# A hybrid attention step on one core: forgetting and differential score tasks mixed, gate products spread by VectorE's work, first attention pieces loaded early

## Chip, cores and metric

One NeuronCore of a Trainium2 chip runs the whole kernel. The metric is the device time of one execution in microseconds; lower is better. All operands are float32; matrix products are made of three products of halves (a high part, which the array takes without loss, and the low rest), so that one product of 128x128 by 128x512 appears as three matmuls.

## The reference

One decoder layer for a prompt of 2048 rows and for 8 sampled sequences of 4 rows. The prompt's part that matters here:

```python
q_a, k_a, v_a, gate_a, q_b, k_b, v_b, f_b, gate_b, m_a, m_b = split(h @ w_in)
# differential attention: 4 heads, two maps each, 64 wide, causal, linear position bias
s = einsum('bqmhd,bkmhd->bmhqk', q, k) * DH_A ** -0.5
p = softmax(where(dist >= 0, s - slopes * dist, NEG_INF))
p = p[:, 0] - lam * p[:, 1]
o_a = einsum('bhqk,bkhd->bqhd', p, v)
# forgetting attention: 8 heads, 64 wide, causal, bias from sums of log forget values
s = q @ k * DH_B ** -0.5 + F_q - F_k
o_b = softmax(where(causal, s, NEG_INF)) @ v
y = (sigmoid(m_a) * y_a + sigmoid(m_b) * y_b) @ w_o     # gates: columns of h @ w_in
```

## The kernel before, in words

The stages follow one another: `head` and `project` twice (one per half of the rows) make queries, keys, values and part of the gates. Then come `gates_and_maps`, `attention_a` (differential), `attention_b` (forgetting), `sample` and `merge`. The change lies in `gates_and_maps` and in the start of `attention_a`.

`gates_and_maps` (L1660) does three things at once. **Gate products:** six chunks of 512 columns by eight row tiles of 128, 24 matmuls each (L2115), 1152 in all; ScalarE copies a finished tile out of one of two PSUM banks `z` (L1922) and issues its store (L1930). Weights of a chunk come in two halves, `front` (two places) and `back` (one place). **Forgetting tasks,** 192 of them: a score tile of 128 rows by up to 1024 columns (L2068, one matmul per 512 columns) of which only the row maximum is kept, by VectorE: L1982 for whole tiles, L1979 with the causal mask for diagonal ones. **Differential tasks,** 192 of them, over 64 map rows (4 heads by 16 row tiles): for map m = 0 and 1 the score tile of each half kh of the keys (L2086 and L2087, two matmuls per 512 columns), its maximum (L1993, L1996), the exponentials on ScalarE (L1942), the row sums' factor (L2003 to L2007), and the difference p0 - factor x p1 (L2016), which SyncE stores to DRAM as the final map (L1834). A row tile of the first eight has one half, the others two.

Score tiles live in six PSUM banks; a tile of 1024 columns takes two. A bank of a forgetting tile comes free with its maximum, one of a differential tile with its exponential. TensorE works through the products in order, and each task has a written-out due product (`due`): the task's matmuls are issued before that product. Before the change all forgetting tasks come first, then all differential ones, and `due` comes from a small model of VectorE's pace (`dve_of`, `paced`). ScalarE follows the same due times, VectorE the order of tasks. The difference of map row g-1 stands behind the maximum of task (m = 1, kh = 0) of row g.

SyncE issues all loads and the maps' stores in one order, written per forgetting segment of eight tasks and per map row: weights that are due, keys and queries for later tasks (after a wait for the scores that used their places), then the stores of the previous row's map pieces (after the wait for its difference). Map pieces p0 have a ring of five, p1 of two.

`attention_a` (L2123) loads each map again in 40 blocks of 512x512 (L2166; a diagonal block in four copies, 640 KB; another 1 MB) into eight places, turns them on TensorE (L2263), splits them in high and low parts on ScalarE (L2225) and VectorE (L2247), and multiplies by the values (L2283, L2284, L2290). An output of four tiles is scaled (L2239) and stored. Its SyncE queue also loads values (`load_v`, 1 MB per part) and the first two units of `attention_b` (`load_b`, 3.1 MB each, behind blocks 8 and 14).

## Time and profile before

| | us |
|---|---|
| runs (median of 3) | 2637.28 (2634.48 to 2637.7) |
| profiled execution | 2636.46 |
| its span in the trace | 2634.8 |
| `gates_and_maps` (first product to last) | 943.6 to 1551.7 |
| `attention_a` up to the first score of `attention_b` | 1551.7 to 1762.3 |

The span is that of the engines' instructions; the profiled execution took 1.7 us more.
### The profile page before, as it was taken

What the parts mean: (1) busy time and instruction counts of PE and PEld (TensorE: products, weight loads), DVE (VectorE), ACT (ScalarE), POOL (GpSimd) and SP (SyncE); (2) the same over time, 40 slices, a digit from 0 to 9 for tenths busy, and PEclk for the clock granted to TensorE, in tenths of its full rate; (3) what the DMA queues carried; (4) which work ended last, traced back from release to release, by engine and by line L of the source; (5) the groups of instructions that cost most, each with busy time, mean ns of one, the idle gap of its engine ahead of it and who ended that gap; (6) DMA issues with size and microseconds to landing.
All of it is one profiled execution on the core that took longest, in us unless ns stands there. A gap on an engine that the chain in (4) does not pass through costs nothing. (4 is left out here: it accounts for less than half of the span.)

```text
span 2634.8 us, 34403 instructions
## 1 busy us (share of the span) xinstructions
PE 2447.5 (93%) x12466; PEld 1942.9 (74%) x12466; DVE 1549.1 (59%) x2701; ACT 837.6 (32%) x1445; POOL 185.4 (7%) x182
## 2 busy tenths in 40 slices
PE   6999999999999999999887677999999987999998
PEld 2788888887788877887665456887777754788886
DVE  3412246634666258887678744557787755655564
ACT  4211122234323210034444433444444433321221
POOL 1000122201222000000000011000000000000000
PEclk8999999999999999999995569999999999999999
DMA  8644645464454563456664569943546298554542
GB/s 315 232 162 173 213 124 170 153 216 157 142 157 125 202 200 129 142 185 211 208 205 138 165 194 287 322 137 77 123 97 138 88 339 293 173 143 152 154 126 65
DMA packets 323812, 463.19 MB, mean 176 GB/s; under 512 B 61929, under 2 KB 201073, under 8 KB 312574
## 3 DMA queue, kind: packets, MB, share of 16 engines
q1 hardware_dynamic: 309810, 419.79, 52.2%
q10 hardware_dynamic: 12800, 41.36, 4.1%
q8 instruction: 87, 1.43, 0.2%
q0 software_dynamic: 1056, 0.13, 0.1%
q14 instruction: 59, 0.48, 0.1%
HBM read 288.15 MB, written 173.04 MB: 175 GB/s over the span
## 5 line engine op out<-in xcount | busy, mean ns | idle before, releaser
L709 PE MATMUL proj_z<-first_km,h_hi 128*128 128x512 f32 x576 | 231.0, 401 | 3.2 <-DVE first_v L1274 3.2
L1942 ACT ACTIVATE max_p<-max_s_ps,max_neg_top 128x1024 f32<-128x1024 f32 (+4 forms) x192 | 164.7, 862 | 198.9 <-DVE max_neg_top L1993 149.6
L709 PE MATMUL proj_z<-first_km,h_lo 128*128 128x512 f32 x576 | 227.5, 395 | 0.0
L709 PE MATMUL proj_z<-first_v,h_hi 128*128 128x512 f32 x576 | 227.3, 395 | 0.0
L2086 PE MATMUL max_s_ps<-max_k,max_q 128*128 128x512 f32 (+3 forms) x320 | 148.3, 465 | 73.8 <-ACT max_p L1942 42.5
L709 PE MATMUL proj_z<-proj_w_hi,h_hi 128*128 128x512 f32 x512 | 203.2, 397 | 0.0
L709 PE MATMUL proj_z<-proj_w_hi,h_lo 128*128 128x512 f32 x512 | 199.9, 390 | 0.0
L709 PE MATMUL proj_z<-proj_w_lo,h_hi 128*128 128x512 f32 x512 | 199.3, 389 | 0.0
L2385 ACT ACTIVATE att_b_pf<-att_b_s_ps 128x1024 f32<-128x1024 f32 (+2 forms) x160 | 142.6, 898 | 101.1 <-PE att_b_s_ps L2428 77.6
L2402 DVE TENSOR_TENSOR att_b_p_lo<-att_b_pf,att_b_p_hi 128x1024 fp32r<-128x1024 f32 (+2 forms) x160 | 170.5, 1066 | 5.5
L2086 PEld LDWEIGHTS max_s_ps<-max_k,max_q 128*128 128x128 f32 x320 | 76.6, 240 | 111.6 <-ACT max_p L1942 59.4
L2087 PE MATMUL max_s_ps<-max_km,max_qm 70*128 70x512 f32 (+3 forms) x320 | 140.8, 450 | 0.0
L2397 DVE CAST att_b_p_hi<-att_b_pf 128x1024 fp32r<-128x1024 f32 (+2 forms) x160 | 98.0, 613 | 68.8 <-ACT att_b_pf L2385 66.3
L2247 DVE TENSOR_TENSOR att_a_p_lo<-att_a_turned,att_a_p_hi 128x512 fp32r<-128x512 f32 (+3 forms) x160 | 93.5, 607 | 74.5 <-ACT att_a_p_hi L2225 74.0
L1049 POOL TENSOR_TENSOR proj_rstd<-proj_rstd,keep_neg_half 128x8 f32<-128x8 f32 (+1 forms) x68 | 112.6, 1655 | 325.4 <-DVE proj_rstd L1372 325.4
L709 PEld LDWEIGHTS proj_z<-first_km,h_hi 128*128 128x128 f32 x576 | 108.4, 188 | 28.9 <-issue 5.0
L709 PEld LDWEIGHTS proj_z<-first_km,h_lo 128*128 128x128 f32 x576 | 108.3, 188 | 25.6
L709 PEld LDWEIGHTS proj_z<-first_v,h_hi 128*128 128x128 f32 x576 | 108.5, 188 | 23.9
L1240 ACT ACTIVATE proj_work<-proj_z 128x512 f32<-128x512 f32 x64 | 38.2, 597 | 272.8 <-PE proj_z L709 272.8
L1370 DVE TENSOR_REDUCE proj_ss<-proj_work 128x8 f32<-128x512 f32 (+1 forms) x68 | 46.6, 685 | 124.2 <-ACT proj_work L1241 124.2
L1979 DVE CUSTOM_DVE_ANT_0 max_s_ps<-max_s_ps,max_causal 128x128 f32<-128x128 f32 (+7 forms) x128 | 95.5, 778 | 32.9 <-PE max_s_ps L2068 32.4
L2225 ACT ACTIVATE att_a_p_hi<-att_a_turned 128x512 fp32r<-128x512 f32 (+3 forms) x160 | 83.6, 534 | 97.4 <-PE att_a_turned L2263 96.6
(451 smaller groups left out, 5790.5 us busy)
## 6 DMA issues: line engine op xcount, KB each, us to landing
w_raw<-in_w_in SPq DMA_DIRECT2D x144, 256.0 KB, 3.8
att_a_maps<-scratch_maps SPq DMA_DIRECT2D x24, 1024.0 KB, 10.1
scratch_maps<-max_p SPq DMA_DIRECT2D x40, 512.0 KB, 2.7
smp_v_a<-scratch_mixes SPq DMA_DIRECT2D x16, 1024.0 KB, 5.1
first_km<-scratch_w_split SPq DMA_DIRECT2D x9, 1024.0 KB
first_v<-scratch_w_split SPq DMA_DIRECT2D x9, 1024.0 KB
head_w<-in_w_ada SPq DMA_DIRECT2D x8, 1024.0 KB, 6.6
scratch_mixes<-proj_out SPq DMA_DIRECT2D x32, 256.0 KB, 3.5
```

The source lines that it names most:

```text
L709: ins = nc.tensor.matmul(out, left(*lt), right(*rt), start=first and n == 0, stop=last and n == len(terms) - 1)
L1049: nc.gpsimd.tensor_tensor(rstd[0:pn, :], rstd[0:pn, :], k.neg_half[0:pn, :], ALU.pow).then_inc(rstd_done, 1)
L1370: step.inc(nc.vector.reduce_sum(ss[0:pn, :], si.rearrange("p (u d) -> p u d", d=DH), AX.X))
L1942: nc.scalar.activation(dst, scores(x), ACT.Exp, bias=neg_top[:, g % 4, m, both:both + 1], scale=-1.0 if kh == qt // 8 else 1.0, accum_out= ...
L1979: nc.vector.tensor_tensor_reduce(s, s, causal[:, 1024 - w:1024], -1.0, -NEG, ALU.add, ALU.min, accum_out=to).then_inc(max_done, 1)
L2086: nc.tensor.matmul(o, q2[:, y % 3, m, at:at + P], k2[:, p, m, s0:s0 + w], start=True, stop=False)
L2087: last = nc.tensor.matmul(o, qm[0:AQ, y % 3, m, at:at + P], km[0:AQ, p, m, s0:s0 + w], start=False, stop=True)
L2225: nc.scalar.activation(p_hi[:, n % HR, 0:w], turned[:, n % PLACES, 0:w], ACT.Copy).then_inc(hi_done, 1)
L2247: nc.vector.tensor_tensor(p_lo[:, n % HR, 0:w], turned[:, n % PLACES, 0:w], p_hi[:, n % HR, 0:w].bitcast(F32), ALU.subtract).then_inc(lo_d ...
L2385: nc.scalar.activation(pf[:, n % PR, 0:w], s_ps[:, n % PLACES, 0:w], ACT.Exp).then_inc(p_done, 1)
L2397: nc.vector.tensor_copy(p_hi[:, n % HR, 0:w], pf[:, n % PR, 0:w]).then_inc(hi_done, 1)
L2402: nc.vector.tensor_tensor(p_lo[:, n % HR, 0:w], pf[:, n % PR, 0:w], p_hi[:, n % HR, 0:w].bitcast(F32), ALU.subtract).then_inc(split_done, 1)
```

## The change

Tasks are mixed: each map row takes 3 or 4 forgetting tasks between its own, in their old order, until four rows before the end, so the last four rows have none. `due` becomes a share of the sum of max(VectorE's, TensorE's) microseconds of the tasks' maxima and scores, without the differences, from product 24 to product 1104 of 1152. Banks are assigned by a small model of when they come free. Gate weights come in quarters (five places), and the tile pairs at a chunk's ends take quarters in turn. The stores of gate tiles move from ScalarE's queue to SyncE's. The difference of row g-1, kh = 0, moves up behind the first task of row g. The forgetting maxima of the two halves are chained through the instruction's start value, and two instructions that joined them go. Forgetting queries are loaded per four tasks. The places of maps, keys, queries and probabilities are laid out anew, so that the first four map blocks can be loaded from `gates_and_maps`; the values of the first head too. `load_b` of unit 0 moves to block 32, that of unit 1 to the start of `attention_b`. The maps' p0 ring is four, p1's three. Position rows of both maps come in one copy.

```diff
-    tasks = b_tasks + a_tasks[:TURN - NBT] + [("t", 0, 0, 0, 0)] + a_tasks[TURN - NBT:]
+    for g, (h, qt) in enumerate(rows):
+        share = min(len(b_tasks), (g + 1) * len(b_tasks) // (NG - 4)) - taken
+        for m in range(2):
+            for kh in range(qt // 8 + 1):
+                tasks.append(("a", g, qt, m, kh))
+                spread = (m, kh) != (0, 0) or qt < HALF
+                for _ in range(min(share, 1) if spread and (m, kh) != (1, qt // 8) else share if (m, kh) == (1, qt // 8) else 0):
+                    tasks.append(b_tasks[taken])
+                    taken += 1
+                    share -= 1
+    tasks.append(("t", 0, 0, 0, 0))
...
-    due, spent = [], 0.0
-    for n, at in enumerate(paced(low)):
-        due.append(min(int((at - spent) / PRODUCT), (NP - TAIL) * EACH))
-        spent += pe_us[n]
+    FIRST, TAIL, PRODUCT = 24, 48, 0.227
+    dve_us = [(0.26 if diagonal(x) else 0.16) + w * 1.05e-3 for x, w in enumerate(width)]
+    pe_us = [(2 if task[0] == "a" else 1) * (w / 2400 + 0.02) for task, w in zip(tasks, width)]
+    load = [max(d, p) for d, p in zip(dve_us, pe_us)]
+    due = [FIRST + int(sum(load[:x]) / sum(load) * (NP * EACH - TAIL - FIRST)) for x in range(N)]
...
-    in_chunk = [(0, 0), (1, 0), (0, 1), (1, 1)] + [(j, half) for j in range(2, T - 2) for half in range(2)]
-    in_chunk += [(T - 2, 1), (T - 1, 1), (T - 2, 0), (T - 1, 0)]
-    NP, EACH = len(pieces), 3 * KD // 2
+    pair = lambda j: [(j + i, q) for q in range(4) for i in range(2)]
+    in_chunk = pair(0) + [(j, q) for j in range(2, T - 2) for q in range(4)] + pair(T - 2)
+    NP, EACH = len(pieces), 3 * KD // 4
...
 (SyncE, per map row g)
+                    if g:
+                        sp.wait_ge(s_done, x)
+                    while next_bq < len(at_b) // 4 and at_b[4 * (next_bq - 2) + 3] < x:
+                        load_bq(sp, next_bq)
+                        next_bq += 1
...
+                    while release < len(released) and (released[release] + 1) * EACH <= due[x]:
+                        follow(release)
+                        release += 1
+                    while done < NZ and any(n == done and (p + 1) * EACH + 4 <= due[x] for p, n in ends.items()):
+                        store(done)
+                        done += 1
                     if g:
                         store_map(g - 1)
...
+                store_map(NG - 1)
+                sp.wait_ge(s_done, N)
+                maps_stored(k, sp, 1)
+                for b in range(MAPS_EARLY):
+                    load_maps(k, sp, b)
...
 (ScalarE)
-                    if finished is not None:
-                        store(finished)
...
 (VectorE)
-                        if m and g and kh == 0:
-                            factors(g - 1)
-                            finish(g - 1, [0] if qt >= HALF else [0, 1])
-                        if m and g and kh == 1:
-                            finish(g - 1, [1])
+                        if g and (m, kh) == (0, 0):
+                            factors(g - 1)
+                            combine(g - 1, 0)
+                        if g and (m, kh) == (1, 0) and rows[g - 1][1] >= HALF:
+                            combine(g - 1, 1)
...
+                dve.wait_ge(exp_done, n_a)
+                nc.vector.reciprocal(k.scale_a[:], sums[:, :, :, 0])
...
 (attention_a, SyncE)
-                    load_block(b)
-                    if b == 1:
-                        load_v(k, sp, 0, LO)
-                    if b == 3:
-                        for part in (HI, LO):
-                            load_v(k, sp, 1, part)
-                    if b == PIECES:
-                        load_b(k, sp, 0)
-                    if b == PIECES + 6:
-                        load_b(k, sp, 1)
+                    if b >= MAPS_EARLY:
+                        load_maps(k, sp, b)
+                    if b in (MAP_PLACES - 1, MAP_PLACES):
+                        load_v(k, sp, 1, b - MAP_PLACES + 1)
...
+                    if b == len(blocks) - 8:
+                        load_b(k, sp, 0)
```

## Rows read from the trace of the kernel before

**Rows 1.** The page: TensorE's busy time over the span, and its clock by slices.

```profile
PE 2447.5 (93%) x12466; PEld 1942.9 (74%) x12466; DVE 1549.1 (59%) x2701; ACT 837.6 (32%) x1445; POOL 185.4 (7%) x182
...
PEclk8999999999999999999995569999999999999999
```

**Rows 2.** Windows of the stage of gates and maps: whole, first half, second half.

```profile
943.60:1551.70 608.10, 530.22 (x2113) 418.70 (x2113) 465.08 (x899) 201.65 (x434) 1.24 (x2) 0.85 0.54 173
943.60:1157.50 213.90, 211.29 (x934) 173.21 (x935) 173.87 (x319) 14.41 (x25) 1.24 (x2) 0.98 0.48 154
1157.50:1538.50 381.00, 305.80 (x1133) 235.21 (x1132) 285.52 (x569) 184.74 (x403) 0.00 (x0) 0.78 0.57 183
```

**Rows 3.** Windows of shorter stretches of the same stage.

```profile
1050.00:1100.00 50.00, 50.00 (x226) 41.11 (x226) 43.33 (x80) 3.59 (x6) 0.00 (x0) 1.00 0.46 159
1100.00:1157.50 57.50, 57.50 (x261) 47.34 (x261) 49.26 (x96) 3.65 (x7) 0.00 (x0) 1.00 0.38 134
1157.50:1200.00 42.50, 42.50 (x196) 35.33 (x195) 36.19 (x79) 25.84 (x56) 0.00 (x0) 1.00 0.59 183
...
1320.00:1350.00 30.00, 30.00 (x140) 24.96 (x139) 24.70 (x46) 16.09 (x36) 0.00 (x0) 1.00 0.56 191
...
1400.00:1450.00 50.00, 36.10 (x90) 25.45 (x89) 40.84 (x77) 24.48 (x54) 0.00 (x0) 0.50 0.47 160
```

**Rows 4.** Waits in the stage: who waited for whom, total us, times, longest.

```profile
PEld max_s_ps L2086 <- ACT max_p L1942: 59.4, 40, 4.5
DVE max_s_ps L1993 <- PE max_s_ps L2087: 55.1, 32, 8.9
ACT max_p L1942 <- DMA scratch_maps<-max_p: 43.0, 5, 11.3
...
PEld max_s_ps L2086 <- DMA max_qm<-scratch_pick_rows: 32.7, 3, 11.8
```

**Rows 5.** Timeline of SyncE's queue at a new head: start, us, issue.

```profile
1253.15 1.26 SPq L1812 DMA_DIRECT2D max_k<-scratch_k_hi  x2
...
1264.39 1.66 SPq L1834 DMA_DIRECT2D scratch_maps<-max_p  x3
```

**Rows 6.** Groups of instructions: busy us, mean ns, idle before.

```profile
L1942 ACT ACTIVATE max_p<-max_s_ps,max_neg_top 128x1024 f32<-128x1024 f32 (+4 forms) x192 | 164.7, 862 | 198.9 <-DVE max_neg_top L1993 149.6 <-DMA scratch_maps<-max_p 43.0 <-DVE max_p L2016 5.1
...
L2016 DVE SCALAR_TENSOR_TENSOR max_p<-max_p,max_factor 128x1024 f32<-128x1024 f32 (+4 forms) x96 | 93.0, 972 | 2.2
...
L2005 DVE RECIPROCAL scale_a<-max_sums 128x2 f32<-128x2 f32 x64 | 10.4, 163 | 1.2
```

**Rows 7.** Timeline: VectorE's first maximum, first map load of the attention, first transposes.

```profile
953.83 0.30 DVE L1979 CUSTOM_DVE_ANT_0 max_s_ps<-max_s_ps,max_causal 128x128 f32<-128x128 f32 x1 [11.97 <-PE max_s_ps L2068]
...
1554.47 3.65 SPq L2166 DMA_DIRECT2D att_a_maps<-scratch_maps  x8
...
1559.64 2.40 PE L2263 MATMUL att_a_turned<-keep_ident,att_a_maps 128*128 128x128 f32 x10 [8.01 <-DMA att_a_maps<-scratch_maps]
```

**Rows 8.** Timeline of the longest stall of the differential attention: TensorE, then VectorE.

```profile
1614.13 0.80 PE L2290 MATMUL att_a_acc<-att_a_p_lo,first_v 128*128 128x512 f32 x1 [11.83 <-DVE att_a_p_lo L2247]
...
1612.79 0.69 DVE L2239 TENSOR_TENSOR att_a_o<-att_a_acc,scale_a 128x512 f32<-128x512 f32 x1 [14.56 <-DMA scratch_o_a<-att_a_o]
```

**Rows 9.** Windows of the differential attention.

```profile
1559.60:1762.20 202.60, 174.72 (x1088) 150.68 (x1088) 103.29 (x176) 91.63 (x176) 17.54 (x33) 0.91 0.91 266
...
1554.40:1735.00 180.60, 149.84 (x935) 129.86 (x936) 87.79 (x152) 78.88 (x154) 18.14 (x33) 0.89 1.01 297
...
1675.00:1750.00 75.00, 75.00 (x504) 65.82 (x503) 47.65 (x82) 42.26 (x83) 0.00 (x0) 1.00 0.83 259
```

**Rows 10.** Instructions on the second unit's places: durations, first and last start.

```profile
L2427 PE MATMUL att_b_s_ps<-map_q x160: 276/394/446, 1805.5 to 2097.7; 128*128 128x512 f32 x112, 128*128 128x384 f32 x16, 128*128 128x256 f32 x16, 128*128 128x128 f32 x16
```

**Rows 11.** Timeline of two gate products in a row at clock 0.50.

```profile
1539.08 0.63 PE L2115 MATMUL max_z<-h_lo,first_km 128*128 128x512 f32 x1
...
1539.51 0.63 PE L2115 MATMUL max_z<-h_hi,first_v 128*128 128x512 f32 x1
```

More of the change, by code:

```diff
@@ L1685, in gates_and_maps @@
+    assert taken == len(b_tasks)
+    tasks.append(("t", 0, 0, 0, 0))
+    N, TURN = len(tasks), len(tasks) - 1
+    at_map = {(g, m, kh): x for x, (kind, g, qt, m, kh) in enumerate(tasks) if kind == "a"}
+    at_b = [x for x, task in enumerate(tasks) if task[0] == "b"]
+    rank_b = {x: r for r, x in enumerate(at_b)}
     order, n_a = [], 0
@@ L1744, in gates_and_maps @@
[L1744 to L1754 removed]
+    FIRST, TAIL, PRODUCT = 24, 48, 0.227
+    diagonal = lambda x: tasks[x][4] == tasks[x][2] // 8
+    dve_us = [(0.26 if diagonal(x) else 0.16) + w * 1.05e-3 for x, w in enumerate(width)]
@@ new lines, in store, with follow @@
+                def store(n):
+                    c, j = n // T, n % T
+                    dst, col = gw.chunks[c]
+                    r = row0 + j * P
+                    to = gate_place(k, row0, j) if c == TURNED else dst[r:r + P, col:col + 512]
+                    sp.wait_ge(z_read, n + 1)
+                    sp.dma_start(to, out[:, n % R, :]).then_inc(stored[n % R], 16)
+                def follow(release):
+                    c, q = release // 4, release % 4
+                    if q < 3:
+                        sp.wait_ge(quarter_read, 3 * c + q + 1)
+                    else:
+                        sp.wait_ge(z_done, (c + 1) * T)
+                    if q < 3 and c + 1 < NC:
+                        load_quarter(k, sp, c + 1, q + 1)
+                    elif q == 3 and c + 2 < NC:
+                        load_quarter(k, sp, c + 2, 0)
+                    elif (c, q) == (NC - 2, 3):
+                        load_v(k, sp, 0, LO)
+                    elif (c, q) == (NC - 1, 1):
+                        load_v(k, sp, 0, HI)
@@ L1884, in _ @@
[L1884 to L1894 removed]
+                    load_q(sp, piece)
@@ L2091, in turn @@
                     free(x)
-                    pe.wait_ge(neg_done, 2)
-                    nc.tensor.transpose(scores(x), shift[:].rearrange("p u t -> p (u t)"), k.ident[:]).then_inc(s_done, 1)
+                    pe.wait_ge(max_done, at_b[-1] + 1)
+                    nc.tensor.transpose(scores(x), neg_top_b[:].rearrange("p u t -> p (u t)"), k.ident[:]).then_inc(s_done, 1)
                 x = 0
                 h_parts = [k.h_hi, k.h_lo]
-                for p, (c, j, half) in enumerate(pieces):
+                for p, (c, j, q) in enumerate(pieces):
                     n = c * T + j
@@ L2137, in attention_a @@
     starts = [0] + [n + 1 for n in ends[:-1]]
-    copies = [4 if kg == g else 1 for h, g, kg in blocks]
     with ExitStack() as ctx:
```

448 lines of the change are left out of this document (188 added, 260 removed).

## Prediction, made before the changed kernel ran

> **What bounds the kernel now.** I first read the page's busy shares: TensorE is busy for 93% of the span, and the slices show where it is not: the second half of the stage of gates and maps and the start of the first attention, with a TensorE clock down to 0.5 [rows 1]. The change touches these two stages alone, so the next view is the windows of the first, 943.6 to 1551.7 us. Over its 608.1 us VectorE is busy 465.08 us and ScalarE 201.65 [rows 2]. It has two halves. Until 1157.5 the forgetting scores run, and TensorE is busy 211.29 of 213.90 us; from there to 1538.5 the differential maps run, and it is busy only 305.80 of 381.00 us at a mean clock of 0.78 [rows 2].
>
> TensorE's true need comes from the stretches where it was busy throughout at clock 1.00: 226, 261, 196 and 140 matmuls in 50, 57.5, 42.5 and 30 us [rows 3], 823 in 180 us, or 0.219 us each. The stage's 2113 matmuls [rows 2] are then 462 us. VectorE needs 465 and TensorE 462, but one after the other: products are spent early (none between 1400 and 1450, where 90 score matmuls took 50 us at clock 0.50, [rows 3]), and VectorE is idle for 143 us. The waits say on what: on TensorE's scores (55.1 us of it before one line alone). TensorE in turn waits 59.4 us for an exponential to free a bank of scores and 32.7 us for pieces of queries. ScalarE waits 43.0 us for stored maps [rows 4]. The last two are one stall, at each new head: SyncE issues keys and queries from 1253.15 to 1264.39 us before it can store a map [rows 5], while the ring of map pieces is full; it comes at three heads.
>
> **Mixed order.** No matmul, reduction or exponential is removed. Each of 64 map rows (4 or 2 score tasks) gets three or four forgetting tasks between its own, until row 60; the last four rows have none. Products are spread by the larger of VectorE's and TensorE's work per task, without the differences (93.0 us, [rows 6]); as these go evenly with the map rows, the shares hold. Small edits of VectorE, together: two shift instructions (0.2 us each) go, one reciprocal is added, 64 others halve their width, at a cost set by the issue and not the width (0.163 us for two columns, [rows 6]). I count 0, between -1 and +1. The floor is therefore VectorE's 465 us, plus a lead and a tail. Lead: it now starts 10.2 us after 943.6 (at 953.83, [rows 7]); the first score will need keys and queries of a map, and four small loads go ahead: twelve DMAs from about 945 on, at 0.5 to 0.6 us of issue each, are issued by 951.7 and have to land, so 12 (10 to 16). Tail: 48 products, 10.5 us, follow the last score, beside some 5 us of VectorE; so 6 without VectorE. Floor: 483.
>
> How close VectorE gets to 100% is what the trace does not show. The nearest rows: 49.26 of 57.50 us = 0.86 and 24.70 of 30.00 = 0.82, both with TensorE as the limit; 40.84 of 50.00 = 0.82 with banks as the limit at half clock [rows 3]. The forgetting tasks hold their banks only until the reduction (and they are a good third of VectorE's work, 173.87 us before 1157.5, [rows 2]), so the mixture presses less on six banks than maps alone. Between 0.82 and 1.0 I take 0.92, halfway in time: 465 / 0.92 + 18 = **523 us, 85 less**. At 0.82 it is 585 (23 less), at 0.97 it is 497 (111 less).
>
> **What can hold it up**, inside that 0.92. Score tiles of the gates: pieces are now quarters (6 products, not 12), and at three places of each of six chunks a tile starts 6 products after another has ended, 1.3 us, and needs its copy. That copy stands on ScalarE behind exponentials that wait for maxima: a reduction (1.22 us) and an exponential (0.86) more, less the 1.3, with the copy itself up to some 2.5 us each, 18 times 45 us if none were hidden, 0 if VectorE still has scores to reduce. Copies' stores go from ScalarE's queue to SyncE's: 48 issues of 0.34 us; the ring of three covers about 30 us, one row of maps delays them by some 8. SyncE waits at each row for its first score, then issues queries (four DMAs for five), forgetting queries for four tasks (once per 1.25 rows), gate weights in 40 half-sized loads for 20, then waits for the previous row's difference. Behind that wait stand the next row's loads and stores. From a row's first score to the use of its forgetting queries four to eleven tasks pass, 3 to 14 us of VectorE; where only four, a late SyncE shows. At a head's start it issues twelve key loads (fifteen before), some 8 us, but rows are now about 6 us and not 3, so the ring of four fills later. I expect 2 to 4 us three times instead of some 10 each.
>
> **Start of the first attention.** Now it needs 210.6 us from 1551.7 to 1762.3. TensorE first waits to 1559.64 for map pieces issued at 1554.47 [rows 7]. Its longest later wait is 11.83 us at 1614.13, behind VectorE, whose own wait was 14.56 us for a stored output [rows 8]; over 180.6 us the DMA share is 1.01 at 297 GB/s, and 1088 matmuls take 202.6 us, 27.9 of them idle [rows 9]. At 504 in a fully busy 75 us [rows 9] they are 162 us. The change loads four map blocks (three of 640 KB, one of 1 MB, 2.9 MB) and the rest of the first values (1 MB) ahead of the stage, moves the second unit's 3.1 MB behind it and the first unit's 3.1 MB from the 9th block to the 33rd of 40. Of some 54 MB 7.0 leave: the DMAs need 182 x 0.87 = 159 us, as long as TensorE. Early copies stand behind the last map's store and TensorE's last score, 10.5 us before the stage's end, so two or more blocks are there at the start. Best end: 162 + 3 = 165; worst: only the first wait goes, 203. I take **176, 35 less**, nearer the best because the long stalls sit where the moved 6 MB were in the queue. The second unit's loads now open the second attention; its first use was 43 us after that stage's start (1762.3 to 1805.5, [rows 10]). Cost 0; without that cover, their 10 us.
>
> **Sum.** Profiled execution 2636.46 us (span 2634.8): 2636.5 - 85 - 35 = 2516. The median of the runs is 0.8 above it, so **2517**.
>
> **Rivals.** *Coupled* (0.22): banks, copies and SyncE's order hold VectorE at 0.82 even in the mixture; 585 and 176 give 2636.5 - 23 - 35 = 2579. For it: 0.82 to 0.86 is all that VectorE ever showed in this stage. Against: TensorE or half clock was the limit then.
>
> *DMA-bound attention* (0.15): loads stay the limit, or the early ones come late; 523 and 203 give 2544. For it: 1.01 of share now.
>
> *Half clock, slower than before* (0.04). In the rows the clock is 0.50 where TensorE did 90 matmuls in 50 us, 40% of its rate, and 1.00 where it was busy [rows 3]. If waits for banks, now spread over the whole stage, brought the low level (1.2 GHz) for a share s of TensorE's work, each product there takes 0.43 us from start to start (1539.08 to 1539.51, [rows 11]) for 0.23: need 462 x (1 + 0.87 s). From s = 0.45 on (643 us) the stage eats the attention's 35 us too; at s = 0.6 it is 703 + 18 = 721 us and the kernel 2714. Against: TensorE's work is 462 of 523 us, 88%, with no long pause planned.
>
> The Trainium skill, "TensorE: Matmul & The Clock Gate", section "A second HAM failure mode: psum-queue depth-cycling", tells of a kernel whose short waits for banks between groups of matmuls made the clock swing between its levels although each was brief. By that rule this rival would be the outcome of mixing; by the rows it needs far lower activity. So far the trace bears the rows out: from 1157.5 to 1200 the same scores, exponentials and products ran together at 1.00.
>
> *Forecast* (0.57): 2517. The remaining 0.02 is a plan that cancels itself, within 0.2% (5 us, about what a measurement of this kernel can tell from no change). Range: low end with shares of 0.97 and attention 45 less, 2480; high end the coupled case, 2580. Faster 0.94, same 0.02, slower 0.04.
>
> **What would show it.** Right: the stage ends at 1450 to 1485; VectorE's share in it is 0.88 to 0.90 and TensorE's clock above 0.95 throughout; no stretch without products; waits of ScalarE for stored maps under 15 us; the first transposes within 2 us of the attention's start; the attention's DMA share over 0.9 but TensorE idle under 15 us. Wrong: waits for ScalarE's copies or for exponentials of over 60 us on TensorE (coupled); waits for forgetting queries; clock digits of 5 to 8 in the stage (half clock); idle time of the attention unchanged at 28 us (DMA-bound).

## The result, and the profile after

The changed kernel takes 2622.8 us, the median of 7 runs (2618.03 to 2629.03); the kernel before, measured beside it, 2637.7 (7 runs, 2633.62 to 2639.52). The ratio is 0.9947, with a 95% interval from 0.9933 to 0.9961: faster by 15 us (0.5%), where 120 were forecast. The sign was right. The time lies above the whole range of 2480 to 2580, and above the rival called coupled (2579).

The two profiled executions differ by 13.6 us of span (2634.8 and 2621.2), and the stages add up to it:

| stretch | before | after | difference | forecast |
|---|---|---|---|---|
| gates and maps (first to last product) | 608.1 | 626.6 | +18.5 | -85 |
| from there to the first transposes | 7.9 | 9.5 | +1.6 | |
| differential attention, first transposes to the second attention | 202.7 | 173.3 | -29.4 | |
| the last two together | 210.6 | 182.8 | -27.8 | -35 |
| the rest (mostly the second attention and the merge) | 872.5 | 867.8 | -4.7 | 0 |
| start of the stage | 943.6 | 944.0 | +0.4 | 0 |

So the smaller term nearly held. The larger one came out with the other sign: mixing the tasks, as it was done, made its stage longer. The page's busy line and clock, to be held against [rows 1]:

```profile
PE 2430.4 (93%) x12466; PEld 1918.9 (73%) x12466; DVE 1548.1 (59%) x2700; ACT 838.0 (32%) x1445; POOL 185.7 (7%) x182
...
PEclk8999999999999989989899999999999999999999
```

The slices at 5, 5 and 6 are gone. By the clock alone one would call the stage repaired. Windows of the stage (whole, the two halves at the places of [rows 2], 50 us of it) and of the differential attention say otherwise; the columns are those of [rows 2]:

```profile
944.00:1570.60 626.60, 523.92 (x2113) 403.32 (x2113) 463.69 (x898) 202.25 (x433) 1.25 (x2) 0.93 0.56 172
944.00:1157.50 213.50, 175.82 (x700) 136.88 (x701) 149.57 (x304) 62.76 (x137) 1.25 (x2) 0.90 0.59 172
1157.50:1540.00 382.50, 321.35 (x1307) 245.87 (x1306) 295.33 (x556) 126.58 (x266) 0.00 (x0) 0.94 0.56 175
1400.00:1450.00 50.00, 39.68 (x164) 30.81 (x163) 37.23 (x83) 13.86 (x38) 0.00 (x0) 0.90 0.60 165
1580.10:1753.40 173.30, 168.10 (x1088) 146.04 (x1088) 103.20 (x176) 91.58 (x176) 18.37 (x34) 0.98 0.91 277
```

The work is what it was: 2113 matmuls, 463.69 us of VectorE (465.08 before). Its share is 0.70 in the first half, which holds the lead without VectorE (0.74 without these 11.5 us), and 0.77 in the second; before, the second half with maps alone had 0.75, and the first half with forgetting tasks alone 0.81 [rows 2]. So the mixture levelled the halves, but below their mean: 0.74 over the whole. The forecast's 0.92 was a share without lead and tail. Set against it stands 463.69 / 607.4 = 0.76, where 607.4 is 626.6 less a lead of 11.5 us and a tail of 7.7. The waits of the stage say what VectorE stands for (who waits for whom, total us, times, longest); [rows 4] is the same view:

```profile
DVE max_neg_top L1994 <- PE max_s_ps L2075: 64.9, 55, 2.2
PEld max_s_ps L2056 <- DMA map_region<-scratch_q_hi: 35.7, 7, 10.6
DVE max_s_ps L1991 <- PE max_s_ps L2075: 32.9, 34, 13.2
PE max_s_ps L2056 <- DMA map_region<-scratch_q_hi: 32.8, 7, 10.2
PE max_s_ps L2074 <- DVE max_neg_top_b L1977: 29.5, 23, 2.4
...
PE max_s_ps L2074 <- DVE max_neg_top_b L1980: 21.8, 18, 1.9
```

L1977 and L1980 are the maxima of forgetting tasks, L1991 and L1994 those of map tasks, L2056 and L2074/L2075 the scores of the two kinds. In place of 42.5 us in which TensorE's matmuls waited for exponentials (59.4 at the weight loads, [rows 4]), it waits 58.8 us for **forgetting maxima** (29.5 + 21.8, and 7.5 before L2056), in 58 waits; the waits for exponentials are down to 4.5. And 32.8 us, in seven waits, are for forgetting queries. ScalarE's waits for stored maps fell from 43.0 to 22.5 us.

**The banks.** One of the 58, in order of time, with TensorE, VectorE and ScalarE around it (start, us, engine, instruction, idle before and who ended it):

```profile
1174.56 1.28 DVE L1991 CUSTOM_DVE_ANT_0 max_s_ps<-max_s_ps,max_causal,max_neg_top 128x1024 f32<-128x1024 f32 x1
...
1175.76 0.86 DVE L1977 CUSTOM_DVE_ANT_0 max_s_ps<-max_s_ps,max_causal 128x640 f32<-128x640 f32 x1
1175.94 1.12 ACT L1942 ACTIVATE map_plain<-max_s_ps,max_neg_top 128x1024 f32<-128x1024 f32 x1 [4.84 <-DVE max_neg_top L1991]
...
1176.74 0.50 PE L2074 MATMUL max_s_ps<-map_region 128*128 128x512 f32 x1 [1.39 <-DVE max_neg_top_b L1977]
...
1177.04 1.11 ACT L1942 ACTIVATE map_plain<-max_s_ps,max_neg_top 128x1024 f32<-128x1024 f32 x1
...
1177.99 1.23 DVE L1994 TENSOR_REDUCE max_neg_top<-max_s_ps 128x1 f32<-128x1024 f32 x1 [1.30 <-PE max_s_ps L2075]
```

A late row has four score tasks of 1024 columns, two for each map, and each takes a pair of the six banks. The first map's two tasks hold two pairs from their scores until the exponentials, which can't begin before both maxima are there (1175.94). The third pair is all that is left, and the forgetting task that was put behind them has it. TensorE can't start the second map's scores until that task's maximum is taken: it stands 1.39 us. VectorE has then nothing to reduce until those scores are written: it stands 1.30. One pair for three tasks makes the two engines work in turns. Of line L1994's 55 waits, 36 (48.6 of its 64.9 us) are for scores whose own start had just waited for a forgetting maximum; counted in the timelines of the two engines over the stage. In the order before, the third pair was empty at this place.

**The queue.** Timeline of SyncE's queue at a new head, and of TensorE:

```profile
1264.94 0.47 SPq L1799 DMA_DIRECT2D map_region<-scratch_q_hi  x1
1265.45 1.25 SPq L1822 DMA_DIRECT2D map_region<-scratch_k_hi  x2
...
1274.75 0.49 SPq L1814 DMA_DIRECT2D map_region<-scratch_pick_rows  x1
...
1277.57 0.47 SPq L1799 DMA_DIRECT2D map_region<-scratch_q_hi  x1
...
1280.18 0.47 SPq L1799 DMA_DIRECT2D map_region<-scratch_q_hi  x1
...
1286.85 1.22 PE L2056 MATMUL max_s_ps<-max_bk,map_region 66*128 66x512 f32 x2 [10.19 <-DMA map_region<-scratch_q_hi]
```

L1799 loads forgetting queries, L1822 and L1814 a head's keys and queries. Twelve key loads, four of queries, two of gate weights and the stores stand between the load at 1264.94 and the next at 1277.57. The ring of forgetting queries holds two pieces of four tasks, so TensorE goes on for eight tasks at most and then stands, here 10.19 us. Most of that lies behind the issue, not before it: the DMA engines are full with the loads issued ahead, and the load of 1277.57 can be used only at 1286.85. A window of this stretch, in the columns of [rows 2]:

```profile
1277.50:1286.80 9.30, 0.00 (x0) 0.00 (x0) 0.48 (x1) 0.67 (x2) 0.00 (x0) 0.63 1.06 332
```

**The ends of the stage** (VectorE's first maximum; then TensorE and SyncE's queue at the stage's end):

```profile
955.51 0.30 DVE L1991 CUSTOM_DVE_ANT_0 max_s_ps<-max_s_ps,max_causal 128x128 f32<-128x128 f32 x1 [13.23 <-PE max_s_ps L2075]
...
1570.21 0.40 PE L2100 MATMUL max_z<-h_hi,first_v 128*128 128x512 f32 x1
...
1570.92 0.60 SPq L1627 DMA_DIRECT2D first_v<-scratch_v_hi  x1
1571.63 6.58 SPq L1918 DMA_DIRECT2D scratch_neg_max<-map_region  x2
1578.26 1.40 SPq L1850 DMA_DIRECT2D scratch_gates_bT<-max_out  x3
...
1580.11 2.15 PE L2235 MATMUL att_a_turned<-keep_ident,map_region 128*128 128x128 f32 x9 [9.50 <-PEq L1824]
```

The first transposes don't wait for maps (the trace names no DMA as their releaser). They stand behind 9.5 us in which SyncE issues two small stores (6.58 us) and three gate stores (1.40 us); the program's next part starts when these are issued.

### The profile page after: what moved, and what is told of

Same layout as the page of the kernel before. It is cut to its first block and busy times, and to the rows that moved or that the text cites. A ratio compares the mean times of both kernels' runs of the same rounds, so it can differ in the third digit from the quotient of the medians.

```text
span 2621.2 us, 34524 instructions
## 1 busy us (share of the span) xinstructions
PE 2430.4 (93%) x12466; PEld 1918.9 (73%) x12466; DVE 1548.1 (59%) x2700; ACT 838.0 (32%) x1445; POOL 185.7 (7%) x182
## 5 line engine op out<-in xcount | busy, mean ns | idle before, releaser
L2074 PE MATMUL max_s_ps<-map_region 128*128 128x512 f32 (+3 forms) x320 | 124.9, 390 | 58.1 <-DVE max_neg_top_b L1977 29.5
L2358 ACT ACTIVATE map_plain<-att_b_s_ps 128x1024 f32<-128x1024 f32 (+2 forms) x160 | 142.4, 898 | 102.0 <-PE att_b_s_ps L2401 77.5
L2375 DVE TENSOR_TENSOR att_b_p_lo<-map_plain,map_region 128x1024 fp32r<-128x1024 f32 (+2 forms) x160 | 170.5, 1066 | 5.5
L1942 ACT ACTIVATE map_plain<-max_s_ps,max_neg_top 128x1024 f32<-128x1024 f32 (+4 forms) x96 | 82.6, 863 | 231.6 <-DVE max_neg_top L1991 209.1
L2056 PE MATMUL max_s_ps<-max_bk,map_region 66*128 66x512 f32 (+2 forms) x320 | 105.8, 397 | 40.8 <-DMA map_region<-scratch_q_hi 32.8
L2370 DVE CAST map_region<-map_plain 128x1024 fp32r<-128x1024 f32 (+2 forms) x160 | 98.1, 613 | 67.9 <-ACT map_plain L2358 65.5
L1942 ACT ACTIVATE max_second<-max_s_ps,max_neg_top 128x1024 f32<-128x1024 f32 (+4 forms) x96 | 82.6, 863 | 154.8 <-DVE max_neg_top L1991 154.7
L2074 PEld LDWEIGHTS max_s_ps<-map_region 128*128 128x128 f32 x320 | 63.8, 199 | 90.7 <-DVE max_neg_top_b L1980 26.8
L2430 PE MATMUL att_b_acc<-map_region,first_v 128*128 128x512 f32 (+1 forms) x320 | 121.1, 379 | 0.5 <-DVE att_b_p_lo L2375 0.5
L2075 PE MATMUL max_s_ps<-map_region 70*128 70x512 f32 (+3 forms) x320 | 120.4, 383 | 0.0
```

The source lines that it names most:

```text
L1942: nc.scalar.activation(dst, scores(x), ACT.Exp, bias=neg_top[:, g % 4, m, late:late + 1], scale=-1.0 if kh == late else 1.0, accum_out=tot ...
L2056: last = nc.tensor.matmul(scores(x)[:, c0:c0 + w], bq[0:AB, y % 2, at:at + P], bk[0:AB, kh, c0:c0 + w], start=True, stop=True)
L2074: nc.tensor.matmul(o, q2[:, y % 3, m, at:at + P], k2[:, p, m, s0:s0 + w], start=True, stop=False)
L2075: last = nc.tensor.matmul(o, qm[0:AQ, y % 3, m, at:at + P], km[0:AQ, p, m, s0:s0 + w], start=False, stop=True)
L2358: nc.scalar.activation(pf[:, n % PR, 0:w], s_ps[:, n % PLACES, 0:w], ACT.Exp).then_inc(p_done, 1)
L2370: nc.vector.tensor_copy(p_hi[:, n % HR, 0:w], pf[:, n % PR, 0:w]).then_inc(hi_done, 1)
```

## The experiments

All are edits of the changed kernel. The stage and the waits are from one profiled execution of each; of waits the table gives TensorE's for forgetting maxima, exponentials and forgetting queries, and VectorE's for scores, in us.

| kernel | total us (runs) | stage | DVE share | forg. maxima | exponentials | queries | DVE on scores |
|---|---|---|---|---|---|---|---|
| before | 2637.7 (7) | 608.1 | 0.76 | 0 | 42.5 | 31.1 (maps') | 125.6 |
| changed | 2622.8 (7) | 626.6 | 0.74 | 58.8 | 4.5 | 32.8 | 146.2 |
| a1 queries on GpSimd | 2609.3 (1) | 610.2 | 0.76 | 59.0 | 12.5 | 2.3 | 126.1 |
| a2 exponentials free | 2557.7 (1) | 558.8 | 0.82 | 5.7 | 0 | 30.7 | 78.8 |
| a5 both | 2531.4 (1) | 531.2 | 0.86 | 6.0 | 0 | 2.2 | 48.6 |
| a3 tail | 2625.8 (1) | 626.5 | 0.74 | 58.4 | 4.4 | 33.5 | 146.4 |
| a4 unmixed | 2611.5 (1) | 609.2 | 0.76 | 0 | 67.4 | 29.8 | 74.2 |
| b1 = a1 + planner | 2600.5 (1) | 595.1 | 0.77 | 54.9 | 18.6 | 2.4 | 114.1 |
| b2 = a1 + swap | 2602.0 (1) | 599.4 | 0.77 | 58.5 | 11.3 | 2.5 | 113.0 |
| b3 = b1 + swap | 2583.2 (4) | 582.4 | 0.79 | 53.8 | 17.8 | 2.9 | 98.2 |
| b4 unmixed, GpSimd | 2625.4 (9) | 628.2 | 0.74 | 0 | 66.7 | 38.9 | 91.2 |
| d1 = b1 + clump | 2564.8 (4) | 565.7 | 0.81 | 18.7 | 33.9 | 2.4 | 84.6 |
| e1 clump alone | 2604.0 (4) | 604.3 | 0.77 | 14.1 | 37.8 | 29.7 | 122.8 |
| e2 = d1 + swap | 2568.6 (4) | 569.5 | 0.81 | 20.7 | 32.2 | 2.8 | 84.1 |
| e3 = a5 + clump | 2526.8 (3) | 528.6 | 0.86 | 4.2 | 0 | 2.8 | 49.6 |
| e4 unmixed, queries kept | 2581.0 (3) | 581.1 | 0.79 | 0 | 67.1 | 9.8 | 51.4 |
| c1 unit's load early | 2635.2 (1) | 626.6 | 0.74 | 58.6 | 6.0 | 31.9 | 146.2 |
| c2 no early maps | 2628.2 (9) | 628.3 | 0.74 | 58.6 | 5.8 | 33.8 | 147.2 |

Single runs of one kernel lie up to 14 us apart (b4: 2620 to 2634), so differences under 10 us between single runs are read from their stage and waits, not from their totals. The kernel before took 2639.7 us beside a1 to a4 and 2644.8 beside a5, b1, b2 and c1. How far a stage length differs from one execution to the next was not measured.

**a1: forgetting queries' loads on GpSimd's queue.**

```diff
+                for y in range(2, len(at_b) // 4):
+                    pool.wait_ge(s_done, at_b[4 * (y - 2) + 3] + 1)
+                    load_bq(pool, y, bq_next[y % 2])
...
-                    while next_bq < len(at_b) // 4 and at_b[4 * (next_bq - 2) + 3] < x:
-                        load_bq(sp, next_bq)
-                        next_bq += 1
```

> One edit: the forgetting queries' loads go from SyncE's queue to GpSimd's, which waits for nothing but the four scores that used the place. Banks theory (in the mixed stage the four banks of a map row stay held until its exponentials, so the forgetting tasks and TensorE's next scores cycle through the one pair left, and TensorE and VectorE take turns): the 32.8 us that TensorE waits for these queries go, the 59 us that it waits for forgetting maxima stay or grow; the stage (627 us in the changed kernel) shrinks by 20 to 35 us. Queue theory (SyncE's order and the clock that falls after its long stalls are the main loss): the stage falls to 570 us or less, mean clock in it from 0.93 to 0.97 or more.

The stage fell by 16.4 us, and the waits on queries from 32.8 to 2.3. SyncE's queue was a cause, but the gain is half of that wait and less than the 20 to 35 us expected: waits for forgetting maxima stayed (59.0) and those for exponentials rose from 4.5 to 12.5. I read this as cover: while banks are short, part of a wait for queries hides a wait for banks; a5 bears on it. The edit takes the loads out of SyncE's order and out of the backlog behind its key loads at once (they land 4.2 us after their issue, the median); which of the two counts more was not tried apart.

**a2: exponentials read other data.** A map's banks are then free at its maximum, as a forgetting task's are. The exponentials keep their sizes and their places; the maps they store are not the reference's.

```diff
-                    nc.scalar.activation(dst, scores(x), ACT.Exp, bias=neg_top[:, g % 4, m, late:late + 1],
+                    nc.scalar.activation(dst, k.h_hi[:, 0, 0:width[x]].bitcast(F32), ACT.Exp, bias=k.neg_half[:, 0:1],
...
-                        if tasks[y][0] == "a":
-                            pe.wait_ge(exp_done, order[y] + 1)
-                        else:
-                            pe.wait_ge(max_done, y + 1)
+                        pe.wait_ge(max_done, y + 1)
```

(The planner's bank times follow.)

> The exponentials read other data of the same size (part of the input's high half, with a constant bias) in place of the scores, so a differential tile's banks come free with its maximum, as a forgetting tile's do; the bank planner and TensorE's waits follow. The maps are not the reference's. Banks theory: TensorE's waits for maxima fall from 59 to under 20 us, VectorE's waits for scores from 146 to under 90 us, the stage from 627 to 570 us or less. Queue theory: the waits for queries stay and the stage shrinks by under 15 us.

The stage fell by 67.8 us. Its waits:

```profile
PE max_s_ps L2053 <- DMA map_region<-scratch_q_hi: 30.7, 6, 10.2
...
PE max_z L2097 <- ACT max_out L1930: 16.6, 10, 4.8
DVE max_neg_top L1994 <- PE max_s_ps L2072: 11.7, 16, 2.2
```

VectorE's 64.9 us before L1994 are 11.7; the copies of gate tiles, 2.3 us in the changed kernel, now show with 16.6. The length of the hold is the cause of the largest loss. VectorE's busy time reads 456.26 us here and 463.69 in the changed kernel for the same 898 instructions; their durations added up are the same (517.8 and 518.9). The windows count the overlap of neighbours once, so a fuller VectorE shows a shorter busy time, and shares of busy time understate the gain a little.

**a5: a1 and a2 together.**

> Both causes taken away at once: forgetting queries by GpSimd's queue, and exponentials that read other data so that differential tiles hold no bank after their maximum (the maps are not the reference's). If banks and the queue are the whole of what the forecast missed: stage 525 to 540 us (forecast 523), VectorE's share 0.86 or more, its waits for scores under 60 us. If something else holds it (the fixed order of products and scores, the clock): 545 us or more.

The stage is 531.2 us, against 523 forecast and 483 called the floor. So with both causes gone the stage comes within 8.2 us of the forecast. That is close partly by luck: VectorE's busy time shows as 454.95 us and not 465 (the overlap told under a2), and with 18 us of lead and tail taken off its share is 0.89, not 0.92. The two together give 95.4 us, where one by one they gave 16.4 and 67.8: the queue is worth 27.6 once banks don't cover it.

**a3: small stores ahead of the values' load.** In SyncE's program the stores of the turned maxima and of the last gate tiles go before the loads that follow the last gate pieces.

> At the end of the stage SyncE issues the small stores (shifts and the last gate tiles) ahead of the last load of values, which took it 6.6 us to issue. If that issue is what delays the differential attention: its first transposes come some 3 us after the last gate product in place of 9.5, total 5 to 7 us less, and TensorE may wait 1 to 3 us for values. If the stage's end waits for something else: no change.

The gap fell from 9.5 to 4.2 us and the attention grew from 173.3 to 178.2: no gain, where 5 to 7 us were expected. What the tail gives, the late values take: TensorE now waits 5.8 us for them, once.

**a4: the old order of tasks**, all forgetting tasks and then the maps, with the differences counted in the due times; rings, pieces and loads as changed.

```diff
+    tasks = b_tasks + [("a", g, qt, m, kh) for g, (h, qt) in enumerate(rows) for m in range(2) for kh in range(qt // 8 + 1)]
...
+        if kind == "a" and g and (m, kh) == (0, 0):
+            dve_us[x] += 0.6 + 0.06 + 1.07e-3 * wide(rows[g - 1][1], 0)
+        if kind == "a" and g and (m, kh) == (1, 0) and rows[g - 1][1] >= HALF:
+            dve_us[x] += 0.06 + 1.07e-3 * wide(rows[g - 1][1], 1)
```

> The changed kernel with the tasks in the old order (all forgetting tasks first, then the map rows) and with the differences counted in the spread of the products; all else as changed (quarters, stores by SyncE, rings, early loads). If the mixture costs what it brings: stage 600 to 615 us, close to the 608 of before, TensorE near 100% in the first part. If the parts around it (quarters, SyncE's stores, smaller ring) cost something: 620 us or more. If mixing is a gain that other parts eat: 640 us or more.

The unmixed stage was 609.2 us, 17 less than the mixed one. I read this as "mixing itself costs", too early: two edits are in it, and it has 29.8 us of waits on forgetting queries of its own (19 waits: without maps between, two pieces of four tasks don't cover a load).

**b1: the planner counts the differences**, in due times and bank times, on a1. **b2: the second difference ahead of the third task's maximum**, on a1:

```diff
                     if kind == "a":
-                        top_a(x)
+                        if g and (m, kh) == (1, 0) and rows[g - 1][1] >= HALF:
+                            combine(g - 1, 1)
+                        top_a(x)
```

> GpSimd's queue for the forgetting queries as in a1_bq_pool, and the differences (93 us of VectorE with their factors) are counted in the spread of the products and in the bank planner. If the planner puts scores on banks that are not the first to come free because it leaves the differences out: the stage falls from 610 us by 15 us or more and the waits for forgetting maxima from 59 to under 40. If six banks are short whatever the plan: 600 to 615 us.

> a1_bq_pool with one move on VectorE: the second difference of the row before stands ahead of the maximum of the row's third task and not behind it. TensorE waits there for a forgetting maximum, writes the scores, and VectorE waits 1.3 us for them; the difference (0.3 to 1.3 us, 32 times, 24 us in all) would fill that wait. Banks theory: 15 to 30 us less than a1_bq_pool's 610. Rival: the later maximum delays the exponentials and their banks by as much: within 5 us of 610.

15.1 and 10.8 us, with waits for forgetting maxima hardly changed (54.9 and 58.5). For b1 under 40 was expected, so the bank plan as such was not the cause: TensorE's busy time fell by 12.6 us (525.81 to 513.19, mean clock 0.93 and 0.95), which points at the due times, but the two parts of the edit were not tried apart. For b2 15 to 30 us were expected. The swap lets VectorE do a difference of about 1 us where it stood for the scores of the second map.

**c1: the first unit's load back behind the eighth block**, in place of the 33rd of 40.

> The changed kernel with the first forgetting unit's 3.1 MB loaded again behind the 9th block of maps and not the 33rd; the stage of gates and maps is untouched. If the traffic that was moved out of the first half is what freed the differential attention (173.3 us against 202.7 before): 8 to 20 us more there. If the early maps did it: within 3 us of 173.

The attention took 13.2 us more (186.5; 14.5 us of it one wait of TensorE behind VectorE, the kind that took 11.8 before, [rows 8]), the stage nothing:

```profile
1579.80:1766.40 186.60, 169.53 (x1088) 147.56 (x1088) 103.44 (x176) 91.57 (x176) 18.28 (x34) 0.94 0.85 258
```

Less than half of the attention's gain of 29.4 is this move. The DMA share is lower than with the load at its late place (0.85 and 0.91): the same bytes less evenly, not more of them.

**b3: b1 and b2 together. b4: the unmixed order with a1's queue. d1: b1 with each row's forgetting tasks together** behind its last score task. **c2: no early map blocks** (`MAPS_EARLY = 0`). The edit of d1:

```diff
-                for _ in range(min(share, 1) if spread and (m, kh) != (1, qt // 8) else share if (m, kh) == (1, qt // 8) else 0):
+                for _ in range(share if (m, kh) == (1, qt // 8) else 0):
```

> The changed kernel with three of the small edits together: forgetting queries' loads on GpSimd's queue, the differences counted in the planner's due times and bank times, and the second difference ahead of the third task's maximum. Alone, on top of the queue edit (stage 610.2 us), the planner gave 595.1 and the swap 599.4. If the two remove different waits, the stage is 584 us (610.2 - 15.1 - 10.8) and the kernel about 2589. If both only move the same wait (TensorE for a forgetting maximum, 54.9 and 58.5 us in those runs), the better one stands: 593 to 596 and 2599 or so.

> The unmixed order (all forgetting tasks first, then the maps, differences counted in the due times), and the forgetting queries' loads on GpSimd's queue. Unmixed with the loads on SyncE's queue the stage was 609.2 us, with 29.8 us of TensorE's waits on query loads. Bank theory: mixing itself costs, so this beats the mixed kernel with the same queue edit (610.2), and as the planner edit is in it, it also stands against 595.1: 580 to 595 us if the queries' waits go, the kernel about 2585 to 2597. Rival (mixing pays once queues and planner are right): 600 us or more, so slower than 2600.5 of the mixed kernel with both edits. If the 29.8 us were waits for the maps' queries, which stay on SyncE's queue, 605 to 610.

> The mixed kernel with the queue and planner edits (595.1 us), but each map row's three or four forgetting tasks stand together behind the row's last score task, not one between each two. Bank theory: a forgetting task then seldom has to take the only pair of banks left beside two held ones in the middle of a row, and exponentials catch up during the clump; TensorE's waits for forgetting maxima (54.9 us) fall to 20 to 40, with some of it coming back as waits for exponentials inside the row (10 to 25): stage 575 to 597. Rival (spreading is what lets exponentials catch up): waits for exponentials of over 50 us, stage 605 to 625.

> The changed kernel without the four early map blocks (2.9 MB): all blocks are loaded behind the stage's last stores, as before; the rest as changed (first attention 173.3 us and gap of 9.5). If the early blocks cover the first waits, it loses what the kernel before lost at this place, 8 to 12 us: attention 181 to 185, kernel 2631 to 2635. If the attention is bound by its DMAs, 2.9 MB at 297 GB/s are 10 us: the same number, but spread over the stage and with a DMA share over 0.95. If the tail's issues are the limit anyway (the early loads only delay the small stores, 9.5 us of gap), the gap falls by up to 7 and the sum by no more than 2 us: kernel 2621 to 2625.

b3: 582.4 us, 27.8 less than a1, where the two edits alone gave 15.1 and 10.8: they work on different waits. Ratio to before 0.98 (0.9773 to 0.9827).

b4 went against my theory: 628.2 us unmixed, 33 more than the mixed kernel with the same two edits (b1), and its waits on forgetting queries rose to 38.9. "Mixing itself costs" fell. b4 is also 19 us longer than a4, which differs from it only in the queue of these loads; of that 9.1 us are the queries' waits, and TensorE's busy time for the same 2113 matmuls is 11.5 us longer (516.38 and 504.87, mean clock 0.91 and 0.92). Why the queue should bring that stays open, and a4 ran once.

d1: 565.7 us, 29.4 less than b1, by the place of the tasks within a row alone. 2564.8 us (4 runs), ratio to before 0.9723 (0.9699 to 0.9748). Its waits:

```profile
DVE max_neg_top_b L1989 <- PE max_s_ps L2065: 24.7, 15, 7.9
PE max_s_ps L2083 <- ACT map_plain L1951: 14.8, 19, 3.8
...
PE max_s_ps L2065 <- ACT max_second L1951: 13.9, 3, 7.5
DVE max_neg_top L2003 <- PE max_s_ps L2084: 13.9, 27, 1.6
```

L2003 is L1994 of the changed kernel: 13.9 us in place of 64.9 (58.5 in b1). Now the second map's first task finds the third pair empty, and the forgetting tasks behind the row give the exponentials time. Some of it comes back as waits for exponentials, 33.9 us in place of 18.6.

c2: the attention is 171.6 us, the gap 9.8, and the total 2628.2 (9 runs; ratio to before 0.9963, 0.9953 to 0.9974, which overlaps the changed kernel's interval). The four early blocks, 2.9 MB, buy between nothing and some 5 us. The gap is 9.5 us with them and 9.8 without, but it is another wait: with them TensorE waits for SyncE's issues, without them for the maps. The total lies between the two ranges expected.

**e1 to e4** ask what the clump works through, and what the two unmixed runs hid. e1 is the clump alone on the changed kernel, e2 d1 with b2's swap, e3 a5 with the clump. In e4, b4's forgetting queries are loaded twice only and never again (its forgetting maxima are not the reference's).

> The changed kernel with one edit: each map row's forgetting tasks stand together behind the row's last score task (planner and queues as changed). In the planned kernel with the queue edit the same move took the stage from 595.1 to 565.7 us and the waits for forgetting maxima from 54.9 to 18.7. If the place within the row is the cause by itself: 626.6 - 25 to 40 = 587 to 602 us, kernel 2583 to 2598, waits for forgetting maxima 15 to 30 us instead of 58.8, waits on forgetting queries unchanged at 25 to 40. If it needs the planner (which counts the differences) to work: 610 or more, kernel 2606 or more.

> The clumped kernel (queue and planner edits, 565.7 us) with the second difference ahead of the third task's maximum. In the spread order this took 12.7 us more (595.1 to 582.4). In the clumped order the second difference stands between the row's third and fourth score tasks, whose maxima release the exponentials, so the swap delays an exponential by the difference (about 1 us) 32 times: if exponentials are what is late there, 0 to 20 us slower, stage 566 to 586; if it fills a wait of VectorE for scores as in the spread order, 553 to 561 and the kernel about 2555.

> Exponentials read other data, so that a map's banks come free at its maximum (the maps are not the reference's), forgetting queries on GpSimd's queue, and the clumped order. The same with the spread order had a stage of 531.2 us. Bank theory: the order within a row acts only through how long banks are held, so without the holds it makes no difference: 524 to 538 us. Rival (clumping helps by something else, such as fewer changes between the two kinds of task or the differences' places): 30 us less again, 500 to 510.

> The unmixed order with the differences in the planner, and the forgetting queries loaded only twice and never waited for after that (forgetting maxima are then not the reference's). It takes away the 30 to 39 us of waits on forgetting queries, which fall in the unmixed order's first part, where the two pieces of the ring don't cover a load. Mixing pays by itself if this is still slower than the clumped order's 565.7 us: 580 to 600 us expected. If the query ring was all that held the unmixed order back, 560 to 570.

e1: one line brings 22.3 us of stage; 2604.0 us (4 runs), ratio 0.9875 (0.9857 to 0.9893). Waits for forgetting maxima 14.1 in place of 58.8. The stage lies 2 us above the bound I gave and the total 6 above; waits for exponentials came back with more (37.8 in place of 4.5).

```profile
PE max_s_ps L2056 <- DMA map_region<-scratch_q_hi: 29.7, 5, 8.7
PE max_s_ps L2074 <- ACT map_plain L1942: 23.5, 18, 1.8
DVE max_neg_top L1994 <- PE max_s_ps L2075: 22.6, 32, 2.8
```

e2: no gain from the swap here (2568.6 against 2564.8). The wait that it filled in b3 is gone already.

e3: the clump is worth 2.6 us where banks are free at the maximum (531.2 to 528.6), and 22 to 29 where they are not. So nearly all that it brings goes through the holds. Windows of the stage and of 300 us in its middle; the same 300 us of the changed kernel have 229.70 us of VectorE:

```profile
943.90:1472.50 528.60, 492.10 (x2113) 395.20 (x2113) 454.14 (x898) 207.17 (x433) 25.21 (x48) 0.96 0.67 205
...
1100.00:1400.00 300.00, 283.81 (x1241) 228.52 (x1241) 272.04 (x536) 120.79 (x251) 16.00 (x31) 0.98 0.71 221
```

272.04 / 300 is 0.91. That is about the share that the forecast took for the whole stage, and no run with the holds shows it: d1, the best of them, has 245.44 us there.

e4: unmixed with the queries' waits nearly away, 581.1 us. It still waits 67.1 us for exponentials. d1, mixed and clumped, has 565.7. So mixing these tasks is worth about 15 us where it leaves the third pair alone, far from 85. And e4 is 14.0 us shorter than b1 (595.1), mixed by the spread order: once the queries' waits are nearly gone, mixing in that order does cost, as first thought, and b4 hid it behind 38.9 us of them (e4 also has fewer loads of queries, so the 14 us are not mixing alone).

## Why the prediction was wrong

**The step that failed** is the choice of VectorE's share, 0.92 "halfway in time" between 0.82 and 1.0, and the sentence before it: "the mixture presses less on six banks than maps alone". It went by how long a forgetting task holds its banks, not by which banks are free where it is put. Inside a late row it takes the only pair that two held ones leave, and TensorE and VectorE work in turns. Measured: 463.69 / 607.4 = 0.76 without lead and tail, so that the term forecast as 505 us (465 / 0.92) took 607. The lower bound was wrong too. I took 0.82 from the fullest windows [rows 3] and set aside that the maps' half as a whole ran at 0.75 [rows 2], because TensorE or the half clock was the limit there. The clock did recover, to 0.94, and the share was still 0.77.

**Slips in the sum.** Halfway in time between shares of 0.82 and 1.0 (567 and 465 us) is 516 us, a share of 0.90 and not 0.92; the forecast should have been some 10 us later. For the copies, the terms named (1.22 + 0.86 - 1.3 us, and 0.6 for the copy) come to 1.4 us each, not 2.5, and 18 of them to 25 us, not 45. The 643 us at which half clock eats the attention's gain leave out the 18 us of lead and tail, which the 721 us at s = 0.6 hold. None of them explains the miss.

**Shown apart:** holding the banks until the exponentials costs 67.8 us (a2); SyncE's queue 16.4 as things stood, 27.6 once the banks are out of the way (a1, a5). Both gone, the stage is 531.2 us. More than half of the bank loss was the place of the tasks and the planner's times, not the banks' number: of the 79.0 us between a1 (610.2) and a5 (531.2), d1 gets 44.5 with all six banks held as before.

**Forgetting queries.** The prediction counted four to eleven tasks of cover and said that a late SyncE shows where only four are; it gave that no price. It cost 32.8 us of waits. It also put a new head's twelve key loads against the map stores alone, at 2 to 4 us three times, and missed that forgetting queries, with the shorter ring, stand behind the same loads. The map stores themselves held ScalarE for 22.5 us in three waits, 7.5 each and not 2 to 4.

**Held:** VectorE's need (465 forecast, 463.69); the small edits (-1.4 us for all, counted as 0 within 1); the lead, 11.5 us against 12 (955.51 - 944.0); the tail, 7.7 against 6 (VectorE's last work ends at about 1562.9); ScalarE's copies, bounded by 0 and 45 us and at 2.3 in the trace, though they rise to 16.6 where VectorE is fuller (a2).

**Start of the first attention:** 182.8 against 176 (before 210.6), so 27.8 us gained of 35. Its idle time is as forecast: 173.3 - 168.1 = 5.2 us within the attention, 27.9 before. The 6.8 us missing are in the gap: I expected the transposes within 2 us of the stage's end, and they came after 9.5, behind the issues of small stores. a3 shows that this can't be had by order alone. c1 gives 13.2 of the gain to the first unit's load; the early blocks show next to none (c2). The rest was not tried alone; what else left this stage's queue are the second unit's 3.1 MB and the first values, for which TensorE waited 6.1 us before and not at all now:

```profile
PE att_a_acc L2283 <- DMA first_v<-scratch_v_lo: 6.1, 1, 6.1
```

**The second unit's load** shows no cost, as taken: the rest of the kernel took 867.8 us, not more than 872.5.

**The rivals.** *Coupled* named the right places, except the copies, and the wrong size: it held VectorE at 0.82 and gave a stage of 585 us. The mixed kernel with its banks held came under that only with three more edits (b3, 582.4). *DMA-bound attention* did not come: 5.2 us idle. *Half clock* did not either: mean 0.93 with no slice of the stage under 8, and 524 us of TensorE, less than before. The Trainium skill's "TensorE: Matmul & The Clock Gate", section "A second HAM failure mode: psum-queue depth-cycling", describes short waits for banks that bring the clock down. The trace doesn't bear that out here: this kernel has 58 waits for forgetting maxima, none over 2.4 us, and its mean clock in the stage was 0.93, above the 0.85 before. What the missing 0.07 costs was not tried apart: TensorE is busy 523.92 us in this stage and 492.10 in e3 (mean clock 0.96) for the same 2113 matmuls.

## What to carry to other kernels

When tasks of two kinds are mixed to level two engines, level the buffers too: draw, for each place in the order, who holds which banks and until which instruction, and put the short task where the long holders are finished, not in their midst. Don't forecast for the mixture a share of busy time above what the worse half shows (here 0.75) without a row that shows which of its limits goes away. And a wait that is covered by another is worth less when removed first: the queue was worth 16 us before the banks, 28 after.

## What was not expected of the hardware

TensorE's mean clock in the stage rose from 0.85 to 0.93 and the time rose as well, for TensorE was idle 102.7 us (626.6 - 523.9) and only 77.9 before (608.1 - 530.2). A mean clock is no measure of the loss. Issuing two small stores took SyncE 6.58 us behind 13 loads of maps and the 1 MB load of values (1571.63). With the values' load moved behind them (a3) the same two took 1.35 us, right behind the maps' loads, and with no maps' loads ahead, the values' load issued 5.6 us before (c2), 0.80. So neither alone shows it. Elsewhere one store's issue took 0.32:

```profile
1320.91 0.32 SPq L1841 DMA_DIRECT2D scratch_maps<-map_plain  x1
```

The best version found is d1, at 2564.8 us: 2.8% under the kernel before (interval 2.5 to 3.0%) and 58 us under the changed one.
